# Fourier stage of a three-layer transformer: VectorE scales the turned queries, a chunk of weights is converted behind them, and the mixers' last products take their banks from fixed halves

## The reference

```
h = rms_norm_2(x, mix_norm)
u = h @ w_in                                # 512 x 1280
f_out = fourier_mixer(u[..., :512])         # 4 groups of 128: real(fft2) over positions and channels, then @ fnet_w + fnet_b
q, k, v = the rest of u                     # 8 query heads, 2 key heads of 64
q = rope(rms_norm_2(q, q_norm)); k = rope(rms_norm_2(k, k_norm))
p = softmax(q @ k.T / 8)                    # per head, 512 x 512, no mask
x = x + concatenate([f_out, p @ v], -1) @ w_out
```

## Time and profile before

| | |
|---|---|
| median of 3 runs | 2763.21 us (2760.78 to 2764.92) |
| profiled execution, its own time | 2759.89 us |
| its span | 2758.1 us |
| PE busy | 2715.3 us (98%) |
| DVE, ACT, POOL busy | 1341.8, 899.4, 145.4 us |
| mean granted TensorE clock | 0.995 of 2.4 GHz |

### The profile page before, as it was taken

One profiled execution on the slowest core, in us unless ns is written; L12 is line 12 of the kernel. 1 busy time (PEld: TensorE's weight loads), 2 busy tenths in 40 slices (PEclk: granted clock), 3 DMA queues, 4 the chain that ended last, 5 costly groups with the idle time before them and its releaser, 6 DMA issues.

```text
span 2758.1 us, 31285 instructions
## 1 busy us (share of the span) xinstructions
PE 2715.3 (98%) x12528; PEld 2256.4 (82%) x12528; DVE 1341.8 (49%) x1901; ACT 899.4 (33%) x1283; POOL 145.4 (5%) x140
## 2 busy tenths in 40 slices
PE   8999999999999999999999999999999999999998
PEld 7888878878888888888888888888878888888786
DVE  5444358654443444434555444344443468644433
ACT  4232226543322323322223332232322237432221
POOL 0000004300000000000000000000000054000000
PEclk9999999999999999999999999999999999999999
DMA  4333332023332333323332333233332321233222
GB/s 156 100 93 96 97 89 73 25 90 94 105 96 93 99 100 95 100 93 99 92 99 92 94 105 96 93 100 99 95 92 88 93 75 39 62 106 99 85 91 74
DMA packets 282065, 252.28 MB, mean 91 GB/s; under 512 B 8257, under 2 KB 278721, under 8 KB 281921
## 3 DMA queue, kind: packets, MB, share of 16 engines
q1 hardware_dynamic: 281920, 250.29, 29.6%
HBM read 248.16 MB, written 2.10 MB: 91 GB/s over the span
## 4 chain that ended last, share of the span: by engine, by line
PE 82%; issue 13%; DVE 3%; ACT 1%; POOL 0%; DMA 0%; SPq 0%; POOLq 0%; DVEq 0%; ACTq 0%
PE bank L407 27%; PE bank L409 26%; PE bank L408 26%; PE bank L498 1%; DVE wl L1200 1%; DVE X L1209 0%; DVE acc L1209 0%; PE bank L449 0%; PE bank L555 0%; PE bank L556 0%; DVE Xl L1212 0%; DMA raw<-in_ffn_w_gate 0%; ACT Xh L865 0%; ACT Xh L868 0%; POOL g_rq L1782 0%
## 5 line engine op out<-in xcount | busy, mean ns | idle before, releaser
L1200 DVE TENSOR_TENSOR wl<-raw,wh 128x1024 fp32r<-128x1024 f32 (+3 forms) x490 | 573.2, 1184 | 933.7 <-ACT wh L837 933.0
L407 PE MATMUL bank<-Xh,wl 128*128 128x512 f32 (+1 forms) x2544 | 994.6, 391 | 15.4 <-ACT Xh L868 8.5
L409 PE MATMUL bank<-Xh,wh 128*128 128x512 f32 (+1 forms) x2544 | 992.0, 390 | 0.0
L408 PE MATMUL bank<-Xl,wh 128*128 128x512 f32 (+1 forms) x2544 | 991.4, 390 | 0.0
L837 ACT ACTIVATE wh<-raw 128x1024 fp32r<-128x1024 f32 (+3 forms) x490 | 491.4, 1017 | 972.5 <-PE bank L409 966.9
L407 PEld LDWEIGHTS bank<-Xh,wl 128*128 128x128 f32 (+1 forms) x2544 | 476.3, 187 | 120.0 <-issue 14.2
L409 PEld LDWEIGHTS bank<-Xh,wh 128*128 128x128 f32 (+1 forms) x2544 | 476.0, 187 | 102.8
L408 PEld LDWEIGHTS bank<-Xl,wh 128*128 128x128 f32 (+1 forms) x2544 | 476.3, 187 | 101.0
L408 PE MATMUL bank<-Hl,wh 128*128 128x512 f32 (+1 forms) x1056 | 411.0, 389 | 0.0
L407 PE MATMUL bank<-Hh,wl 128*128 128x512 f32 (+1 forms) x1056 | 411.0, 389 | 0.0
L409 PE MATMUL bank<-Hh,wh 128*128 128x512 f32 (+1 forms) x1056 | 410.8, 389 | 0.0
(11 more groups left out here) (280 smaller groups left out, 1580.0 us busy)
## 6 DMA issues: line engine op xcount, KB each, us to landing
raw<-in_ffn_w_gate SPq DMA_DIRECT2D x128, 512.0 KB, 3.6
raw<-in_ffn_w_up SPq DMA_DIRECT2D x128, 512.0 KB, 3.9
raw<-in_ffn_w_down SPq DMA_DIRECT2D x114, 512.0 KB, 3.4
raw<-in_c_w_in SPq DMA_DIRECT2D x24, 512.0 KB, 3.7
raw<-in_w_in SPq DMA_DIRECT2D x10, 512.0 KB, 3.7
raw<-in_ffn_w_down SPq DMA_DIRECT2D x16, 256.0 KB, 2.6
raw<-in_a_w_in SPq DMA_DIRECT2D x8, 512.0 KB, 3.7
raw<-in_a_w_out SPq DMA_DIRECT2D x8, 512.0 KB, 3.4
```

What stands on the lines that cost most here:

```text
L407: e.matmul(o, ll, rh, start=start, stop=False)
L408: e.matmul(o, lh, rl, start=False, stop=False)
L409: i = e.matmul(o, lh, rh, start=False, stop=stop)
L1200: e.tensor_tensor(lo, src, hi.bitcast(F), ALU.subtract).then_inc(wlo.up(("w", n)), 1)
```

## The change

Three things are changed. (1) In the Fourier stage, DVE instead of POOL multiplies the query heads by their scales, two heads at a time between its other work, and the scale itself is computed later. PE turns query heads 0 and 1 behind the first of the four `seq` groups. ACT and DVE convert chunk 14 behind the `seq` results and not ahead of the keys. (2) The fixed banks of the stage are swapped, 0 to 3 with 4 to 7. (3) In both attention mixers, products down 0 to 3 take banks among 0 to 3, and down 4 to 7 and the output of head 7 among 4 to 7; and in `mixer_out` DVE adds product t+1 to X before it writes the low part of tile t and sums its square.

```diff
-            def take(self, name):
-                bank_of[name] = self.free_banks.pop(0)
+            def take(self, name, among=range(8)):
+                bank_of[name] = next(b for b in self.free_banks if b in among)
+                self.free_banks.remove(bank_of[name])
                 return bank_of[name]
-            def leave(self, *late):
-                self.free_banks.sort(key=lambda b: b in late)
...
# second_half, PE
-                    into.append(take(ring[0].take(name), name) if ks[0] == 0 else banks[bank_of[name]])
+                    among = range(4) if pair < 2 else range(4, 8)
+                    into.append(take(ring[0].take(name, among), name) if ks[0] == 0 else banks[bank_of[name]])
...
# output(h, part), PE
+                        ring[0].take(("out", s, h), range(4, 8) if h == 7 else range(8))
...
# mixer_fnet, PE
-                    into = [take(4 * (blk % 2) + t, ("tok", s, blk, t)) for t in range(4)]
+                    into = [take(4 * (1 - blk % 2) + t, ("tok", s, blk, t)) for t in range(4)]
...
-                    turn(4 + p, ("kt", s, p), [gktm[:, t, p].rearrange("p a b -> p (a b)") for t in range(4)])
-                turn_queries(6, 0)
-                turn_queries(7, 1)
-
+                    turn(p, ("kt", s, p), [gktm[:, t, p].rearrange("p a b -> p (a b)") for t in range(4)])
                 over = [chunk() for _ in range(2)]
                 for g in range(4):
...
+                    if g == 0:
+                        turn_queries(2, 0)
+                        turn_queries(3, 1)
...
# mixer_fnet, ACT
-                use(2)
+                use()
...
+                def weighed(g):
+                    w.wait_ge(mm, ("seq", s, g))
+                    copy(gRB[:, g, :], banks[4 + g][:, :], ("seq", s, g))
...
                 w.wait_ge(mm, ("chan", s))
-                for g in range(4):
-                    w.wait_ge(mm, ("seq", s, g))
-                    copy(gRB[:, g, :], banks[g][:, :], ("seq", s, g))
+                weighed(0)
+                queries(2, 0)
+                queries(3, 1)
+                for g in range(1, 4):
+                    weighed(g)
+                use()
...
# mixer_out, DVE
+                def rest(t):
+                    if 0 <= t < 4:
+                        x_low(s, t, gain, "half", s, 7)
+                    if 0 <= t < 6:
+                        x_square(s, t)
                 for mp in range(4):
                     use()
                     for t in (2 * mp, 2 * mp + 1):
                         add_to_x(s, t, banks[bank_of["down", s, t]], ("down", s, t), ("x", s, t))
-                        if t < 4:
-                            x_low(s, t, gain, "half", s, 7)
-                        if t < 6:
-                            x_square(s, t)
+                        rest(t - 1)
...
# mixer_fnet, DVE
-                w.wait_ge(pool, ("rq", s))
-                w.wait_ge(dve, HERE)
-                tt(gsc[:, :, :], grq[:, :, :], bc(gr8[:, :], 2, [128, 4, 8]), ALU.mult, ("sc", s))
...
-                use(2)
+                use()
+                w.wait_ge(pool, ("rq", s))
+                tt(gsc[:, :, :], grq[:, :, :], bc(gr8[:, :], 2, [128, 4, 8]), ALU.mult, ("sc", s))
+                def scale(*heads):
+                    for h in heads:
+                        q = gqtm[:, :, h].rearrange("p t a b -> p t (a b)")
+                        w.wait_ge(pool, ("tok", s, 1 + h // 4, 3))
+                        w.wait_ge(dve, ("sc", s))
+                        tt(q, q, bc(gsc[:, :, h], 2, [128, 4, 128]), ALU.mult, ("scaled", s, h))
...
# mixer_fnet, POOL
-                w.wait_ge(dve, ("sc", s))
-                w.wait_ge(pool, HERE)
-                for h in range(8):
-                    q = gqtm[:, :, h].rearrange("p t a b -> p t (a b)")
-                    tt(q, q, bc(gsc[:, :, h], 2, [128, 4, 128]), ALU.mult, ("scaled", s, h))
```

More of the change, by code:

```diff
@@ L558, in output @@
                 def output(h, part):
-                    bank = take(ring[0].take(("out", s, h)), ("out", s, h)) if part == 0 else banks[bank_of["out", s, h]]
+                    if part == 0:
+                        ring[0].take(("out", s, h), range(4, 8) if h == 7 else range(8))
+                        take(bank_of["out", s, h], ("out", s, h))
+                    bank = banks[bank_of["out", s, h]]
                     lo, hi = 256 * part, 256 * part + 256
@@ L741, in mixer_fnet @@
                 for n in range(2):
-                    proj([(4 + 2 * n + m, ("u", s, 2 * n + m)) for m in range(2)], [128, 128], KT, Xh, Xl, ready, None)
+                    proj([(2 * n + m, ("u", s, 2 * n + m)) for m in range(2)], [128, 128], KT, Xh, Xl, ready, None)
                 mm.also(("xused", s))
@@ L750, in mixer_fnet @@
                     w.wait_ge(dve, ("u", s, g))
-                    bank = take(g, ("chan", s, g))
+                    bank = take(4 + g, ("chan", s, g))
                     for j in range(4):
@@ L1106, in mixer_fnet @@
                     for t in range(4):
-                        bank = banks[4 * (blk % 2) + t]
+                        bank = banks[4 * (1 - blk % 2) + t]
                         w.wait_ge(mm, ("tok", s, blk, t))
@@ L1651, in mixer_fnet @@
                     for t in range(4):
-                        bank, product = banks[4 * (blk % 2) + t], ("tok", s, blk, t)
+                        bank, product = banks[4 * (1 - blk % 2) + t], ("tok", s, blk, t)
                         if blk == 0:
@@ L1727, in mixer_fnet, with weighed_low @@
                     name = ("chan", s, g)
[L1728 removed]
+                    minus(gABl[:, g, :, :], banks[4 + g][:, :].rearrange("p (j c) -> p j c", j=4), gABh[:, g, :, :], name, name,
                           name)
[L1730 removed]
+                use()
[7 more added lines that the diff above has]
+                        tt(q, q, bc(gsc[:, :, h], 2, [128, 4, 128]), ALU.mult, ("scaled", s, h))
+                def weighed_low(g):
+                    name = ("seq", s, g)
+                    minus(gRB[:, 4 + g, :], banks[4 + g][:, :], gRB[:, g, :], name, name, name)
+                scale(0, 1)
                 for p in range(2):
[L1732 removed]
+                    minus(gKT[:, 1, p, :], banks[p][:, :], gKT[:, 0, p, :], ("k", s, 4 * p), ("kt", s, p),
                           *[("k", s, h) for h in range(4 * p, 4 * p + 4)])
[L1734 to L1738 removed]
+                scale(2, 3)
+                weighed_low(0)
+                queries(2, 0)
+                queries(3, 1)
+                scale(4, 5)
+                weighed_low(1)
+                scale(6, 7)
+                weighed_low(2)
+                weighed_low(3)
+                use()
                 def later():
```

31 lines of the change are left out of this document (10 added, 21 removed).

## The result

The changed kernel took **2747.08 us** (median of 4 runs, 2745.52 to 2750.84) where the kernel before took 2761.99 beside it (4 runs, 2760.73 to 2764.92): a ratio of 0.9946, 95% interval 0.993 to 0.9962, or 14.9 us less. 2749 was forecast.

A forecast was written before the change was run, and what follows sets the result against it. PE, busy 98% of the span, was taken as the bound, so only its waits and slow clock could be won. 3.8 + 9.3 + 1.4 = 14.5 us, less half a microsecond, from median 2763.2 gave 2749 us; range 2743.5 to 2757.5.

The forecast's parts named there:

- Part 1: Stage 2's end: bank wait and slow clock go, a new 1.2 us wait for Xl comes; gain 3.8 us.
- Part 2: Fourier stage up to the chan products: 3.3 us won by the last, 1.4 us more if the slow stretch goes.
- The stage's start: Fourier stage's start: the first block takes banks long read, so 1.05 + 0.15 = 1.2 us go.
- The chunk's wait: Fourier stage, u products: PE's 0.56 us wait for weights goes as the scale moves later; 0.7 us.
- The chan wait: Third group of chan products: the 1.24 us wait for its fold falls to 0 to 0.3.
- Part 3: Heads' scaling on DVE: 0.65 us for each of eight instructions, and PE does not wait for heads.
- Part 4: Chunk 14 behind seq: 8.0 us won by the first score; behind it 2.4 go, 1.1 come back, 1.3 stay.
- Part 5: Stage 8's end: the 0.73 us weights wait goes, the 1.50 us Xl wait shrinks to 1.2; gain 1.4 us.
- (a): Rival, 27%: the clock falls all the same, at chan products or behind stage 3's new wait; about 2751 us.
- (b): Rival, 15%: the attention takes the gain back, softmax and DVE deciding when PE passes row block 2; 2754.5 us.
- (c): Rival, 8%: the mixers' ends do not help, DVE's chunks standing ahead of low parts; about 2759 us.
- (d): Rival, 3%: slower, scaling on DVE becomes the bound ahead of the first row maximum; 2769 us.

The follow-up runs named there:

- run 1: The changed kernel measured once more, unaltered (also called again), against the kernel before: 2749.70 us, ratio 0.9949.
- run 4: The changed kernel with the old order in `mixer_out`, low part and sum of squares directly behind each tile's addition: 2749.87 us, ratio 0.9953.
- run 5: The changed kernel with the mixers' last products taking their banks by the old ring order again: 2745.3 us, ratio 0.994.
- run 6: The changed kernel without the swap of the Fourier stage's fixed banks (also called no_swap): 2750.22 us, ratio 0.9951.
- run 9: The changed kernel with the scale `g_sc` computed early as before, DVE still scaling the heads: 2747.47 us, ratio 0.9951.
- run 8: The changed kernel with POOL scaling the heads and `g_sc` computed early again (also called pool_scales): 2755.23 us, ratio 0.9973.
- run 7: The changed kernel with chunk 14 converted ahead of the keys' copies again (also called chunk_ahead): 2752.75 us, ratio 0.9962.
- run 3: The kernel before with the new Fourier stage alone, both mixers' ends as before: 2751.82 us, ratio 0.9962.
- table_early: The changed kernel with one more ACT exponential ahead of the copy of seq 1, to load its table early: 2747.72 us, ratio 0.9944.

## Why the prediction was right

By the time and by its parts: 14.5 us were summed up. Between the profiled executions, 3.44 us are won up to stage 3's 25th product (33.23 against 36.67), 8.76 from there to row block 2 (2288.20 less 2274.56 is 13.64, of which 4.88 stood at 574.87 against 569.99), and 0.99 from there to stage 9's 25th product (2386.45 less 2371.82 is 14.63): 13.2 in all. The other 1.44 of the 14.63 came by chance, with the 3.4 us at half clock that the profiled execution of before has at 472 us. The medians gave 14.9 us, and 14.0 in run 1. What lies above 13.2 can't be told from the draw of the clock. That the sum of 14.5 met the medians so closely is in part luck: by the parts it was 1.3 too high.

- **Part 1, 3.8 forecast, 3.44 measured.** The new wait for Xl is 1.47, not 1.2. The mechanism is only partly as told. The forecast let the banks take the wait away and took Xl for the next thing late. Runs 4 and 5 show that either edit does most of it: DVE's order alone (run 5) gives all of the 3.44, the banks alone (run 4) give 2.41 (36.67 less 34.26). The two do not add up, and beside the order the banks give nothing here.
- **Part 2.** The stage's start, 1.2 forecast: 1.17, and 1.27 by run 6. The chunk's wait, 0.7 forecast: 0.83 by run 9. The chan wait went as forecast, and its slow stretch with it. That POOL beside DVE made the fold late was argued from 1.69 against 0.76 us; runs 8 and 9 show it. The Trainium skill (GPSIMD Engine Reference, 8. Key points) names such contention for VectorE instructions with two SBUF inputs. The pair of runs agrees with it: 1.69 against 0.76 us for the sums, and 0.74 against 0.75 for the step with one input from PSUM.
- **Part 3, 0.65 us a head forecast:** 1.28 for two. PE waits for none.
- **Part 4, 8.0 us by the first score:** 8.22 (2273.29 less 2260.19 is 13.10, less the same 4.88). Run 7 gives 3.80 of it back, about 3.2 of that for the chunk, as summed up.
- **Part 4, behind the first score, 1.3 forecast, 0.54 measured** (13.64 less 13.10). This term was mis-sized: the new waits are 1.30 and 0.79 us where 1.1 was summed. They stand at the turn of head 2 and the product behind it, since the exponentials have to empty their banks, and not only at the row blocks. The chain through POOL was forecast right: 13.7 us, and POOL has row block 2 ready 13.71 us behind the first score (2270.79 + 3.11 less 2260.19). But PE turned row block 2 only at 14.37. What the forecast left out is the link ahead of that, from the first scores' banks to the exponentials, in which a table load of 1.28 us lies. The load was there before the change too (2277.65), when PE itself came late.
- **Part 5, 1.4 forecast, 0.99 measured:** the wait for Xl is 1.47, not 1.2. Run 3 shows a link that the forecast missed: with the new bank ring and without part (3), this end would have lost 2.4 us against before (100.65 against 98.25), and part (3) wins that back too.
- **The rivals.** (a), the clock, did not happen in either profiled execution of the changed kernel. The table shows behind which waits it fell. Behind the 1.24 us wait amid the narrow chan products the clock fell in 3 of 3 profiled executions, and in none of 11 without it; with waits of 3 us and more at the first score in 3 of 3 (in chunk_ahead 1.0 us before the wait was over), and at the mixers' ends in 3 of 3; behind the waits of 1.30 and 0.79 us (1.39 and 0.73 in pool_scales) in 2 of 9; behind that of 1.46 to 1.51 us for Xl in none of 19, and behind that of 1.31 us in stage 2's attention in none of 14. So the length of the wait alone does not tell. (b) came in small: of the 2.4 us that the forecast let go behind the first score, the attention took back 1.9. (c) and (d) did not happen.

## What to carry to other kernels

A wait for a buffer is removed by freeing it earlier as well as by choosing another: try the order of the engine that frees it first, and look which operand is due next. Here the new order alone brought stage 3's 25th product to where both edits bring it, and the new banks alone 1.03 us short of that. Before a chunk conversion or a scale is placed, look what it waits for and what stands behind it; ACT's one chunk held back keys, queries and seq results. If two edits each take a wait away, test them apart and together: here one of them protected a place that the other had spoilt.

## What the runs showed of the hardware

The same wait of 1.96 us at 472 us was followed by 0, 3.4, 6.8 or 10.2 us at 1.2 GHz, in 10 of 14 profiled executions by some of it. Each us of it costs 0.41 to 0.45, from that product to the one behind the 0.75 us wait in the same attention: that takes 59.87 us without a slow stretch, 61.39 with 3.4 us (before), 62.66 with 6.8 (no_swap; 62.63 to 62.69 in the others), and 64.06 or 64.26 with 10.2 (again; pool_scales and table_early). At 10.2 us it is nearly all of the 4.6 us between the two profiled executions of the changed kernel, and most likely the spread of its runs: the two at 2745.5 us had a mean granted clock of 0.998, the two at 2748.63 and 2750.84 had 0.996. Where in those two the clock fell is not shown. A 1.24 us wait between 128-column products was followed by 3.4, 6.8 and 10.2 us in three executions, so the price of one and the same wait, with the clock behind it, went up to 6.3 us (7.09 less 0.83, runs 8 and 9). What decides between these lengths stays open.

The table load took 1.28 us on ACT, and in table_early, with the load moved away, the first exponential came 1.43 us earlier. The Trainium skill (ScalarE: Activation LUTs, What ACT_TABLE_LOAD costs) gives about 1283 ns for the load, and adds a drain of about 1.38 us for every switch to a different set of tables. The load's time agrees. Of the drain no row here shows anything: the load ends at 2265.34, and the exponential begins at 2265.35.
